# Three attention loops: probabilities turned four steps behind the scores, exponentials in the step of the scores

## The reference

```python
# nsa: 16 query heads, 4 key groups; selected blocks (all 8 causal blocks are selected
# at 512 tokens) and a window of 512, besides a small compressed branch
ss = jnp.where(m_sel, einsum('bgrqd,bgqkcd->bgrqkc', qq, k_sel) * scale, NEG)
p_s = jax.nn.softmax(ss, axis=-1)
o_s = jnp.einsum('bgrqkc,bgqkcd->bgrqd', p_s, v_sel)
p_w = jax.nn.softmax(jnp.where(m_w, sw, NEG), axis=-1)
o_w = jnp.einsum('bgrqk,bgkd->bgrqd', p_w, vwb)
return gg[..., 0:1] * o_c + gg[..., 1:2] * o_s + gg[..., 2:3] * o_w

# swa (window 128, 16 heads) and even (|i - j| <= 128, 8 heads): a sink joins the softmax
mx = jnp.maximum(sc.max(axis=-1, keepdims=True), sink)
e = jnp.exp(sc - mx)
p = e / (e.sum(axis=-1, keepdims=True) + jnp.exp(sink - mx))
o = jnp.einsum('bgrnqk,bnkgd->bnqgrd', p, vv)
```

## Time and profile before

| | us |
|---|---|
| median of 3 runs | 2438.16 |
| lowest and highest | 2437.75, 2439.35 |
| profiled execution | 2441.44 |
| its span | 2439.3 |
| TensorE, VectorE, ScalarE, GpSimd busy | 2339.3, 1317.7, 957.6, 318.7 |

### The profile page before, as it was taken

How to read it: one execution, slowest core, us unless ns; L and a number is a source line. 1 busy time by engine, 2 the same in 40 slices (tenths; PEclk the granted TensorE clock), 3 DMA queues, 4 the chain that set the end, 5 groups by cost and what they waited for, 6 DMA issues and landing times.

```text
span 2439.3 us, 30299 instructions
## 1 busy us (share of the span) xinstructions
PE 2339.3 (96%) x11616; PEld 1845.5 (76%) x11616; DVE 1317.7 (54%) x1802; ACT 957.6 (39%) x1401; POOL 318.7 (13%) x255
## 2 busy tenths in 40 slices
PE   9999999999998979999998989999999999999998
PEld 7775567888886657888887767888887757788887
DVE  6448756665545575665456765333346674433333
ACT  4327753443323363443233353322313862333222
POOL 0000003110003013111003014101112002211010
PEclk9999999999999999999999999999999999999999
DMA  5220002222222102222223112222223202222222
GB/s 183 104 70 35 2 18 86 86 103 87 103 90 94 50 36 70 102 103 87 103 86 129 70 49 73 103 89 103 102 86 112 87 1 86 87 104 86 91 104 81
DMA packets 31493, 203.79 MB, mean 84 GB/s; under 512 B 4260, under 2 KB 5288, under 8 KB 7720
## 3 DMA queue, kind: packets, MB, share of 16 engines
q1 hardware_dynamic: 30104, 199.37, 23.0%
q10 hardware_dynamic: 1296, 3.15, 0.3%
HBM read 200.41 MB, written 2.10 MB: 83 GB/s over the span
## 4 chain that ended last, share of the span: by engine, by line
PE 83%; DVE 9%; ACT 5%; issue 2%; DMA 0%; SPq 0%; ACTq 0%; POOLq 0%; POOL 0%; DVEq 0%
PE D L582 72%; PE D L698 3%; PE X L684 2%; PE D L706 2%; DVE w_lo L1649 2%; DVE xg L1683 2%; ACT prob L1313 1%; ACT w_hi L1109 1%; DVE h L1708 1%; DVE prob L1981 1%; PE X L690 1%; PE X L807 1%; ACT xg L1109 1%; DVE prob L1950 0%; ACT mid L1109 0%
## 5 line engine op out<-in xcount | busy, mean ns | idle before, releaser
L582 PE MATMUL D<-xg,w_hi 128*128 128x512 f32 x3184 | 995.6, 394 | 23.8 <-DVE xg L1683 17.3
L582 PE MATMUL D<-mid,w_hi 128*128 128x512 f32 x2308 | 716.4, 392 | 20.4 <-DVE w_lo L1649 9.4
L582 PEld LDWEIGHTS D<-xg,w_hi 128*128 128x128 f32 x3184 | 601.7, 190 | 157.1 <-DVE xg L1683 19.3
L1649 DVE TENSOR_TENSOR w_lo<-w_raw,w_hi 128x2048 fp32r<-128x2048 f32 (+2 forms) x210 | 456.8, 2176 | 362.9 <-ACT w_hi L1109 362.6
L582 PE MATMUL D<-xg,w_lo 128*128 128x512 f32 x1592 | 624.7, 392 | 0.0
L1109 ACT ACTIVATE w_hi<-w_raw 128x2048 fp32r<-128x2048 f32 (+2 forms) x210 | 355.7, 1694 | 487.4 <-PE D L582 482.3
L582 PEld LDWEIGHTS D<-mid,w_hi 128*128 128x128 f32 x2308 | 434.5, 189 | 116.4 <-issue 17.9
L582 PE MATMUL D<-mid,w_lo 128*128 128x512 f32 x1154 | 450.7, 391 | 0.0
L582 PEld LDWEIGHTS D<-xg,w_lo 128*128 128x128 f32 x1592 | 301.8, 190 | 63.9
L582 PEld LDWEIGHTS D<-mid,w_lo 128*128 128x128 f32 x1154 | 217.7, 189 | 45.4
L1708 DVE TENSOR_TENSOR h<-D,h 128x1024 f32 (+1 forms) x71 | 86.8, 1223 | 260.4 <-PE D L582 260.4
...
## 6 DMA issues: line engine op xcount, KB each, us to landing
...
```

What stands on the lines that cost most here:

```text
L582: last = nc.tensor.matmul(out, w[a], x[b], start=start and k == 0, stop=stop and k == 2)
L1649: return nc.vector.tensor_tensor(out, x, f(high), ALU.subtract)
```

## The change

For nsa, swa and even the turn of a unit comes four steps behind its scores in place of three. The exponentials of unit s are issued in ScalarE's step s, behind the copy of unit s-4. VectorE takes the maximum of s first and then scales s-1. There are six probability buffers in place of four, and 16 in place of 8 columns for maxima and sums. Room for them comes from overlays: the zeros `idle_x` for the idle matmuls share a place with `kc_all`, and the last idle matmuls read zeros of `masks`. The odd loop keeps its lags and its order. In nsa's step 3 TensorE no longer waits by name for the copies of the values.

```diff
-EXP_LAG = {"nsa": 1, "swa": 1, "even": 1, "odd": 0}
-LAG = {"nsa": 3, "swa": 3, "even": 3, "odd": 2}
+LAG = {"nsa": 4, "swa": 4, "even": 4, "odd": 2}
...
-            [("under_prob", [P, 8, SEQ], F32), ("prob_4", [P, 4, 2, SEQ], F32)],
+            [("under_prob", [P, 4, SEQ], F32), ("prob_6", [P, 6, 2, SEQ], F32)],
...
-            return prob[:, a % 2] if kind == "odd" else prob_4[:, a % 4]
+            return prob[:, a % 2] if kind == "odd" else prob_6[:, a % 6]
...
                         if g == 3:
                             pe.wait_ge(c_evac, 3)
-                        else:
-                            for v in range(u, u + 2):
-                                pe.wait_ge(d_free[v % 2], v // 2 + 1)
                         compressed_turn(g, D[:, 3, :])
...
-                    if 0 <= s - EXP_LAG[kind] < count:
-                        n = s - EXP_LAG[kind]
-                        a = a0 + n
+                    if s < count:
+                        a = a0 + s
                         c, p = pair_of(a), probs(kind, a)
...
                         act.wait_ge(maxed, a + 1)
...
-                    if kind != "odd" and 0 <= s - 2 < count:
-                        scale_unit(kind, l, units, s - 2)
                     if s < count:
...
-                            if s >= 4:
-
-                                dve.wait_ge(turned, a - 3)
+                            if s >= 6:
+
+                                dve.wait_ge(turned, a - 5)
...
                         ins.then_inc(maxed, 1)
-                    if kind == "odd" and 0 <= s - 1 < count:
-                        scale_unit(kind, l, units, s - 1)
+                    if 0 <= s - 1 < count:
+                        a = a0 + s - 1
+                        t, qt, branch = units[s - 1]
+                        c, w = pair_of(a), len(key_blocks(kind, qt)) * P
+                        dve.wait_ge(exped, a + 1)
+                        nc.vector.reciprocal(inv_sum[:, c:c + 2], row_sum[:, c:c + 2]).then_inc(inverted, 1)
+                        dve.wait_ge(inverted, a + 1)
...
-                        if s >= 4:
-                            pool.wait_ge(turned, a - 3)
-                        nc.gpsimd.tensor_copy(prob_4[:, a % 4, :, w:w + 1],
+                        if s >= 6:
+                            pool.wait_ge(turned, a - 5)
+                        nc.gpsimd.tensor_copy(prob_6[:, a % 6, :, w:w + 1],
```

More of the change, by code:

```diff
@@ L194, in build_program @@
         mla_qn, mla_qr, mla_kn, mla_kr = (normal[x] for x in ("mla_qn", "mla_qr", "mla_kn", "mla_kr"))
-        prob_4 = normal["prob_4"]
+        prob_6 = normal["prob_6"]
         w_raw = [sb(f"w_raw{s}", [P, UNIT]) for s in range(2)]
@@ L270, in build_program @@
         masks = sb("masks", [P, 7, P], BF16)
-        idle_x = sb("idle_x", [P, 2 * P], BF16)
         ssum = sb("ssum", [P, SEQ])
@@ L283, in build_program @@
         lru_work = [gates[:, k // 4, 8 * (k % 4):8 * (k % 4) + 8] for k in range(8)]
-        kc_all = sb("kc_all", [P, NSA_GROUPS, CMP_N])
+        early = overlay([("idle_x", [P, 2 * P], BF16)], [("kc_all", [P, NSA_GROUPS, CMP_N], F32)], size=NSA_GROUPS * CMP_N * 4)
+        idle_x, kc_all = early["idle_x"], early["kc_all"]
         small = overlay([("pos_x", [P, 64 + P], F32R)], [("vc_all", [P, NSA_GROUPS, HD], F32)], size=NSA_GROUPS * HD * 4)
@@ L295, in build_program @@
         block_rstd = sb("block_rstd", [P, QT])
-        neg_max = sb("neg_max", [P, 8])
-        row_sum = sb("row_sum", [P, 8])
-        inv_sum = sb("inv_sum", [P, 8])
+        neg_max = sb("neg_max", [P, 16])
+        row_sum = sb("row_sum", [P, 16])
+        inv_sum = sb("inv_sum", [P, 16])
         lru_c = sb("lru_c", [P, 3, 8])
@@ L613, in project, with keep_busy @@
                 last.then_inc(w_used, 1)
-            def keep_busy(n):
+            def keep_busy(n, zeros):
                 for _ in range(n):
-                    nc.tensor.matmul(X[:, 0, 0:2 * P], idle_x[:, 0:P], idle_x[:, :], start=True, stop=True)
+                    nc.tensor.matmul(X[:, 0, 0:2 * P], zeros[:, 0:P], zeros, start=True, stop=True)
             def norm_sums(norm):
@@ L671, in feed_forward @@
                                 project(u0 + n, x_mid(slot), ks=ks, ends=n == 3)
-                            keep_busy(20)
+                            keep_busy(20, masks[:, 1:3, :].rearrange("p m k -> p (m k)"))
                             continue
@@ L1091, in _ @@
             pe.wait_ge(idle_in, 1)
-            keep_busy(56)
+            keep_busy(56, idle_x[:, :])
             for l, kind in enumerate(layers):
@@ L1299, in attend @@
                         copy(prob_t[:, a % 2, :, 0:w], D[:, 0:2, 0:w]).then_inc(evac, 1)
-                    if 0 <= s - EXP_LAG[kind] < count:
-                        n = s - EXP_LAG[kind]
-                        a = a0 + n
+                    if s < count:
+                        a = a0 + s
                         c, p = pair_of(a), probs(kind, a)
-                        w = len(key_blocks(kind, units[n][1])) * P + (kind in SINK0)
+                        w = len(key_blocks(kind, units[s][1])) * P + (kind in SINK0)
                         act.wait_ge(maxed, a + 1)
                         if kind in SINK0:
-                            act.wait_ge(sink_in, sinks_before[l] + n + 1)
+                            act.wait_ge(sink_in, sinks_before[l] + s + 1)
                         if kind == "odd" and s >= 2:
@@ L1934, in recurrence_step @@
                     gated_low(3)
-            def scale_unit(kind, l, units, n):
-                a = units_before[l] + n
-                t, qt, branch = units[n]
-                c, w = pair_of(a), len(key_blocks(kind, qt)) * P
-                dve.wait_ge(exped, a + 1)
-                nc.vector.reciprocal(inv_sum[:, c:c + 2], row_sum[:, c:c + 2]).then_inc(inverted, 1)
-                dve.wait_ge(inverted, a + 1)
-                for o in range(2):
-                    p = probs(kind, a)[:, o, 0:w]
-                    inv = inv_sum[:, c + o:c + o + 1]
-                    if kind == "nsa":
-                        ins = nc.vector.tensor_scalar(p, p, inv, gate_of(t, o, qt, branch), ALU.mult, ALU.mult)
-                    else:
-                        ins = nc.vector.tensor_scalar(p, p, inv, None, ALU.mult)
-                ins.then_inc(normed, 1)
             def attend(kind, l, u_out, n_late=None, u_late=None):
@@ L1985, in attend @@
                         ins.then_inc(maxed, 1)
-                    if kind == "odd" and 0 <= s - 1 < count:
-                        scale_unit(kind, l, units, s - 1)
+                    if 0 <= s - 1 < count:
[5 more added lines that the diff above has]
+                        dve.wait_ge(inverted, a + 1)
+                        for o in range(2):
+                            p = probs(kind, a)[:, o, 0:w]
+                            inv = inv_sum[:, c + o:c + o + 1]
+                            if kind == "nsa":
+                                ins = nc.vector.tensor_scalar(p, p, inv, gate_of(t, o, qt, branch), ALU.mult, ALU.mult)
+                            else:
+                                ins = nc.vector.tensor_scalar(p, p, inv, None, ALU.mult)
+                        ins.then_inc(normed, 1)
                     if s >= lag + 2 and (s - lag - 2) % per == per - 1:
```

2 lines of the change are left out of this document (1 added, 1 removed).

## The result

| | before | changed |
|---|---|---|
| median of 13 runs, us | 2438.16 | 2449.64 |
| lowest and highest, us | 2436.48, 2442.82 | 2445.63, 2459.26 |
| profiled execution, its span, us | 2441.44, 2439.3 | 2452.83, 2450.7 |

The ratio is 1.0052, 95% interval 1.0043 to 1.0061: the change costs 11.5 us. Forecast were 2452.4 us and a range of 2444 to 2460. The prediction was right in sign and cause, and near in size; several of its terms were off and cancelled in part.

What follows compares the result with a forecast made beforehand. TensorE was taken to bound the kernel (83% of the chain), VectorE the swa and even loops. Terms of 9.2 (nsa), 2.4 (swa), 1.6 (even) and 1.0 (clock) sum to 14.2; 2438.2 + 14.2 = 2452.4 us, range 2444 to 2460.

Steps and rivals of the forecast that it cites:

- nsa, start to the scores of unit 8: nsa's start: compressed norm now waits behind the first scaling, losing its cover, so the next maximum comes later; +1.5 us.
- nsa, scores of unit 8 to scores of unit 56: nsa's steady part: five periods losing 0.7 us each and 1.2 in the one with weight pieces; +4.7 us.
- nsa, from there to the loop's end: nsa's end: one more turn and values behind the last, later scores, and a late copy; +3.0 us.
- swa: swa loop, bound by VectorE: low output halves wait longer for the output copy; 74.1 for 71.7 us, +2.4.
- even: even loop, bound by VectorE, carried through likewise: 47.2 for 45.6 us, +1.6.
- clock: nsa's start: longer TensorE standstill brings the half-rate clock; 0 to +3 us more, +1 taken.
- The path S, M, E, C, T in nsa: nsa: scores, maximum, exponentials, copy, turn for four-block units; stalls of 0.68 and 0.61 us, period 19.31 for 18.64.
- The floor of 1.13 us under a low half's wait: swa: each of six `ao_low` waits for the output copy lasts at least 1.13 us, 6.8 together for 4.4 before.
- The signs: Profile checks: nsa periods 19.3 us, copy waits 16, maximum waits some 20, unit 8 1.5-3 later; swa output-copy waits 11-13.
- Rival 1: Added step frees TensorE: nsa wins 5 us, swa and even about 1 in their starts; 2432 us, chance 0.06.
- Rival 2: A wash: nsa's stalls 0.3 in place of 1.3 us a period; 2438, up to 2442 us, chance 0.06.
- Rival 3: Slower still: low clock stays through nsa's start and returns in swa's tail; +6, 2460 us, chance 0.08.

Runs made afterwards that it cites:

- e1: Changed kernel with ScalarE's exponentials issued one step later, as before the change; 2435.32 us, ratio 0.9991.
- e3: Changed kernel with VectorE scaling s-2 ahead of the maximum of s, and TensorE again waiting for value copies in nsa's step 3; 2465.98 us, ratio 1.0115.
- e4: Changed kernel with turns three steps behind the scores in place of four, everything else kept; 2443.75 us, ratio 1.0022.
- e9: Kernel before, with TensorE's idle stretches at the starts of nsa, swa and even filled with matmuls of zeros; 2437.97 us, ratio 1.0005.
- e8: Changed kernel, with TensorE's idle stretches at the starts of nsa, swa and even filled with matmuls of zeros; 2452.02 us, ratio 1.0057.
- e2: Changed kernel with exponentials one step later and VectorE scaling s-2 ahead of the maximum of s; 2436.30 us, ratio 0.9995.
- e7: As e6, with TensorE's idle stretches at the starts of nsa, swa and even filled with matmuls of zeros; 2424.96 us, ratio 0.9946.
- e6: Changed kernel with exponentials one step later in nsa, swa and even, and scaling s-2 ahead of the maximum in nsa only; 2433.43 us, ratio 0.9980.
- e11: As e7, without the filling in nsa; 2426.96 us, ratio 0.9951.

## Why the prediction was right, point by point

| term | forecast, us | measured in the profiled pair, us |
|---|---|---|
| nsa, start to the scores of unit 8 | +1.5 | +0.05 |
| nsa, scores of unit 8 to scores of unit 56 | +4.7 | +4.0 |
| nsa, from there to the loop's end | +3.0 | +4.2 |
| swa | +2.4 | +3.9 |
| even | +1.6 | +2.5 |
| clock | +1.0 | within the rows above |
| everything else | 0 | -3.2 |
| sum | +14.2 | +11.4 |

- **The path S, M, E, C, T in nsa.** Right, by both stalls (0.70 and 0.63 for 0.68 and 0.61), by the period (19.33 for 19.31) and by e1, e3 and e4, whose periods of 18.16, 20.31 and 18.81 were forecast as 18.1, 20.3 and 18.8 by the same working. Between units 8 and 56 the five regular periods cost 0.69 each; the one with weight pieces is left with 0.5 where 1.2 was put.
- **nsa's start, +1.5 and of the clock's +1.** From the first scores to those of unit 8 the loop takes 200.76 - 183.32 = 17.44 us in the changed kernel and 202.84 - 185.45 = 17.39 before. The wait is there. TensorE in the changed kernel:

```profile
184.43 1.14 PE L683 MATMUL X<-kdup,q_all 64*128 64x256 f32 x8 [0.39 <-DVE neg_max L1957]
189.40 1.11 PE L737 MATMUL D<-ident,c_prob 128*128 128x128 f32 x4 [3.83 <-DVE c_prob L2042]
...
200.76 0.49 PE L683 MATMUL X<-kdup,q_all 64*128 64x128 f32 x4
```

  e9 and e8 hold the old and the changed order with the granted clock at 1.00 over this stretch. In e9:

```profile
184.20 0.71 PE L690 MATMUL X<-kdup,q_all 64*128 64x128 f32 x8
...
199.29 0.49 PE L690 MATMUL X<-kdup,q_all 64*128 64x128 f32 x4
```

  and in e8:

```profile
184.72 0.72 PE L689 MATMUL X<-kdup,q_all 64*128 64x128 f32 x8
...
201.45 0.49 PE L689 MATMUL X<-kdup,q_all 64*128 64x128 f32 x4
```

  15.09 and 16.73 us: the longer standstill (3.83 for 1.3 us) costs 1.6, for the 1.5 forecast. What failed is the clock's term. The low level was to cost more, and it cost less: 17.44 - 16.73 = 0.7 us in the changed kernel, 17.39 - 15.09 = 2.3 before, where 1.8 had been put. It lasts 6 to 7 us in both. In the changed kernel it begins at 188 us, while TensorE still stands, and from 190 to 196 VectorE is busy 5.8 of 6 us, so the slower matmuls delay little; before it lay on work, from 191 to 198, and at its end VectorE stood 1.75 us for exponentials. The sign of the term was wrong in this place.
- **The end of nsa.** +3.0 forecast, +4.2 measured (from the scores of unit 56, at 316.86 before and 318.75 now). The granted clock is 0.66 from 340 to 345, and it falls on work:

```profile
341.61 1.51 PE L697 MATMUL D<-ident,prob 128*128 128x128 f32 x6 [0.98 <-ACT prob_t L1105]
343.06 1.55 PE L705 MATMUL D<-prob_t,vall 128*64 128x128 f32 x12
```

  Such a turn and such values take 0.77 and 0.81 from start to start at full clock and 1.45 and 1.48 here: 1.4 us of the 4.2 is clock, the order's part is 2.8.
- **swa and even.** The floor of 1.13 us under a low half's wait is right: four of the six are 1.05 to 1.17 at full clock, two at low clock 1.36 and 1.72, in sum 7.5 for 6.8. The loops are over by 1.5 and 0.9 us (+3.9 and +2.5 for 2.4 and 1.6), and here is the clock that was put into nsa: 0.91 and 0.96 where it had been 1.00. The forecast argued that swa bears waits in pieces, with 13.0 us of them at a clock of 1.00. It did not bear those of the changed kernel: the clock fell behind waits of 1.05 and 0.68 for maxima at 845, and again at 884, behind waits of 0.99, 0.34 and 1.21.
- **Clock as a whole.** +1 forecast. Loops 14.6 less the 13.2 of order is 1.4. That the two are so near is luck: less clock in nsa's start, more in its end, in swa and in even. Of the distance between 14.2 and the measured 11.5 the larger part lies outside the loops: the stretches there were 3.2 us shorter in the profiled pair, and they vary by more than that between executions.
- **The signs.** Periods, waits for copies, waits for maxima (18.9 us for some 20) and swa's output copies came as said. Unit 8 did not come 1.5 to 3 us later but 0.05.
- **Rival 1** (too few buffers; the Trainium skill, "Perfetto Trace Analysis", section "Optimization Strategy", says that the same gap repeated can mean too few of them) was wrong for this change, yet e2 shows that it had hold of something: with the order of the exponentials left alone, the fourth step and its buffers shorten the period by 0.48 us. Of the 0.6 us a period that the prediction gave it, that is most; and e7, with more than the step changed, has swa 4.6 us shorter than before and even 1.7, where the rival had about 1. **Rival 2** (a wash) fails by the same rows: nsa alone lost 8.2 us. **Rival 3** fits the highest run, 2459.26 us at a mean granted clock of 0.981; where in that run the clock was low no trace shows.
- The rule on gaps and the half-rate clock (the Trainium skill, "TensorE: Matmul & The Clock Gate", section "HAM oscillation"): e7 agrees at swa's start, where filling the gaps takes the granted clock from 0.50 to 1.00, and the program is 8.5 us faster. For the program as a whole e9 does not: its filling took the low clock out of nsa's start and the time stayed.

## What to carry to other kernels

A step added to a software pipeline is worth what it gives the bounding engine, and only if no in-order engine in between has to do newer work ahead of the old: count for each queue how many steps lie between the start of the newest work ahead of an awaited instruction and that instruction. A visible wait that a reordering removes says nothing of the next one; here 5.8 us of one gave way to 11.9 us of another, and three durations (maximum, exponentials, copy), set against TensorE's work beside them, were enough to foresee the period to 0.02 us. Where a pipeline is made deeper, look at its first steps too: the slots left empty there can cost the clock, and idle matmuls can hold it; whether the program gains by that has to be measured.

## What the runs showed that had not been expected

- TensorE fell to 1.2 GHz behind waits as short as 1.05 and 0.67 us, one close behind the other (e6 in swa), and stayed there for some 7 us although it was busy 4.83 of 5 us. In the kernel before waits of 0.84 and 1.14 us at the same place left it at 1.00.
- A spell of 6 to 7 us at 1.2 GHz cost 0.7 us in nsa's start where TensorE stood or VectorE was the busier, 2.3 in the kernel before and 3.3 in e11 (against e7).
- Mean granted clocks of one kernel's runs lie between 0.981 and 0.988 in the changed kernel, and 0.001 goes with about 2 us within one kernel's runs. Between kernels that does not hold: e8 and e9 have a higher mean clock and no gain.
- Fifty idle matmuls, of which ten take 1.27 us, were worth 8.5 us in one kernel (e6 to e7); such fillings were worth nothing in two others (e8, e9).
